# Window columns ahead of gate columns, SSD heads in a row, and banks of row blocks taken one by one, in a two-block kernel on one core

## What is computed

```python
h = modulate_2(rmsnorm(x, norm_mix), shift_m, scale_m)
proj = h @ w_in                                   # 512 pool | 1024 z | 1536 xbc | 16 dt
y_pool = pool_mixer(proj[pool], pool_w, pool_b, pool_scale)   # trailing means over 2, 4, 8, 16 tokens
y_ssd = ssd_mixer(proj[z], proj[xbc], proj[dt], ...)          # short convolution, 16 heads of 64
x = x + gate_m * (concatenate([y_pool, y_ssd]) @ w_out)
h = modulate_2(rmsnorm(x, norm_ffn), shift_f, scale_f)
x = x + gate_f * peer(h, w_query, sub_keys1, sub_keys2, expert_down, expert_up)
...
def pool_mixer(u, pool_w, pool_b, pool_scale):
    mixed = window_sum(u) / count - u
    return (einsum("bsgc,gcd->bsgd", mixed, pool_w) + pool_b) * pool_scale
def ssd_mixer(z, xbc, dt_raw, ...):
    y = ssd_chunked(xs * dt, dt * A, bs, cs) + xs * d_skip    # weights exp(decay) * (c . b) per head
    return rmsnorm(y * silu(z), ssd_norm)
```

## Time and profile before

| | before |
|---|---|
| median of 3 runs | 1455.42 us |
| profiled execution | 1453.92 us |
| its span, first to last instruction | 1452.1 us |
| mean granted TensorE clock | 0.986 |
| share of the span busy: PE, DVE, ACT, POOL | 96%, 71%, 57%, 45% |
| moved by DMA | 284 MB, 196 GB/s |

### The profile page before, as it was taken

The page is one execution under the profiler, slowest core; times in us unless marked ns, Lnnn a source line. Parts: engine busy times, 40 slices in busy tenths (PEclk is TensorE's granted clock), DMA queues, the critical chain, the costliest instruction groups (busy, mean ns, idle before and its releaser), DMA issues.

```text
span 1452.1 us, 31591 instructions
## 1 busy us (share of the span) xinstructions
PE 1400.9 (96%) x9822; PEld 1303.6 (90%) x9822; DVE 1032.7 (71%) x2231; ACT 823.5 (57%) x1602; POOL 649.0 (45%) x499
## 2 busy tenths in 40 slices
PE   5999999999999998999999999999999999999997
PEld 4799999999999968999999999999988888888886
DVE  6777768888867457429999468778775666666665
ACT  6668765555445554547887644334435555555554
POOL 4886791000016737688889866676640000000000
PEclk9999999999999989999999999999999999999999
DMA  8866575888963532564555544344435665655652
GB/s 311 302 230 220 199 264 198 321 318 308 343 238 129 177 106 94 186 224 166 186 183 180 176 141 143 133 144 137 137 126 177 193 196 189 194 195 189 194 194 87
DMA packets 79424, 284.31 MB, mean 196 GB/s; under 512 B 8836, under 2 KB 8964, under 8 KB 79240
## 3 DMA queue, kind: packets, MB, share of 16 engines
q1 hardware_dynamic: 79368, 283.59, 56.8%
HBM read 282.51 MB, written 1.05 MB: 195 GB/s over the span
## 4 chain that ended last, share of the span: by engine, by line
PE 39%; PEld 23%; issue 16%; POOL 16%; DVE 4%; ACT 2%; PEldq 1%; POOLq 0%; DMA 0%; SPq 0%; DVEq 0%; ACTq 0%
POOL w_lo L536 16%; PE psA L1689 9%; PE psA L1693 9%; PE psA L1692 9%; PEld psA L1693 6%; PEld psA L1689 5%; PEld psA L1692 5%; PEld psD L2139 3%; PE psD L1689 3%; PE psD L1692 3%; PE psD L1693 3%; PEld psD L1693 1%; PEld psD L1689 1%; PEld psD L1692 1%; DVE arena L1051 0%
## 5 line engine op out<-in xcount | busy, mean ns | idle before, releaser
L588 ACT CAST w_hi<-raw 128x512 fp32r<-128x512 f32 x872 | 535.3, 621 | 537.2 <-PE psA L1689 406.4
L536 POOL TENSOR_TENSOR w_lo<-raw,w_hi 128x512 fp32r<-128x512 f32 x484 | 642.2, 1345 | 413.9 <-ACT w_hi L588 401.0
L1689 PE MATMUL psA<-h_hi,w_hi 128*128 128x256 f32 x1568 | 453.4, 289 | 0.9 <-POOL w_lo L536 0.9
L1693 PE MATMUL psA<-h_hi,w_lo 128*128 128x256 f32 x1568 | 444.0, 283 | 0.0
L1692 PE MATMUL psA<-h_lo,w_hi 128*128 128x256 f32 x1568 | 444.0, 283 | 0.0
L1008 DVE TENSOR_TENSOR w_lo<-raw,w_hi 128x512 fp32r<-128x512 f32 x388 | 266.9, 691 | 159.5 <-ACT w_hi L588 158.6
L1689 PEld LDWEIGHTS psA<-h_hi,w_hi 128*128 128x128 f32 x1568 | 300.9, 192 | 4.6 <-issue 1.8
L1692 PEld LDWEIGHTS psA<-h_lo,w_hi 128*128 128x128 f32 x1568 | 301.3, 192 | 0.0
L1693 PEld LDWEIGHTS psA<-h_hi,w_lo 128*128 128x128 f32 x1568 | 300.9, 192 | 0.0
L1689 PE MATMUL psA<-w_hi,u_hi 128*128 128x512 f32 x512 | 200.5, 392 | 3.2 <-DVE u_lo L1065 3.2
L1693 PE MATMUL psA<-w_hi,u_lo 128*128 128x512 f32 x512 | 200.1, 391 | 0.0
(11 more groups left out here) (363 smaller groups left out, 2062.6 us busy)
## 6 DMA issues: line engine op xcount, KB each, us to landing
raw<-expert_down SPq DMA_DIRECT2D x128, 512.0 KB, 3.2
raw<-expert_up SPq DMA_DIRECT2D x128, 512.0 KB, 3.5
arena<-ada SPq DMA_DIRECT2D x96, 512.0 KB, 5.1
raw<-gateup SPq DMA_DIRECT2D x44, 512.0 KB, 5.1
raw<-feat SPq DMA_DIRECT2D x28, 512.0 KB, 3.8
raw<-win SPq DMA_DIRECT2D x24, 512.0 KB, 3.2
raw<-down SPq DMA_DIRECT2D x22, 512.0 KB, 6.1
raw<-wout SPq DMA_DIRECT2D x20, 512.0 KB, 4.2
```

The lines of the kernel that those rows point to most:

```text
L536: nc.gpsimd.tensor_tensor(w_lo[:, s * HALF:(s + 1) * HALF], raw[:, n % 8 * HALF:(n % 8 + 1) * HALF], w_hi[:, s * HALF:(s + 1) * HALF].bitc ...
L588: nc.scalar.copy(w_hi[:, n % SLOTS * HALF:(n % SLOTS + 1) * HALF], raw[:, n % 8 * HALF:(n % 8 + 1) * HALF]).then_inc(hi_ready, 1)
L1689: first = mm(o, w[0], m[0], start=start, stop=False, skip_group_check=True)
L1693: return mm(o, w[1], m[0], start=False, stop=stop, skip_group_check=True)
```

## The change

It has four parts. (1) In the first block the convolution of the second pair stands ahead of the reciprocal of the row chain, log1p_exp has one operation fewer, the last rows come behind the third pair, the exp of the row maxima moves on ACT to the head of softmax_exp, and gate_cols moves on PE from behind unit 8 to behind unit 15, with its copy on DVE behind m_decay. (2) row_blocks takes its banks one by one inside the first row block, and ssq_heads comes in the middle of the second row block. (3) ACT splits one half between the normalized blocks of the second block's first norm. (4) The pool columns come ahead of the gate columns. PE runs twelve units with dt_cols and turn_xs behind the first five and the four pooled products behind the last four; then all heads in a row, with two decays ahead of cb and two ahead of each pair. DVE computes sums and means beside the gate columns, and ssd_out writes its sum back to the PSUM bank. The inverse root of the heads goes to PSUM.

```diff
...
-Z2_Z, Z2_POOL = XBC, XBC + KC
+Z2_POOL, Z2_Z = XBC, XBC + NPOOL
...
-            stream(lambda u: win2[u], 24)
+            stream(lambda u: win2[u], XBC)
+            for j in range(NPOOL):
+                load(win2[XBC + KC + j])
 
             sp.wait_ge(d_drained, D_AT["down"] + 4)
             sp.dma_start(pool_wt, pool_w[:, :, :]).then_inc(sem("pool_w_in"), 16)
             sp.dma_start(keysT, keys[:, :, :]).then_inc(sem("keys_in"), 16)
+            stream(lambda u: win2[u + XBC], KC)
...
-            for j in range(2, 7):
+            for j in range(2, 8):
                 qk_bias(j)
-            act.wait_ge(sem("m_rows"), 1)
-            nc.scalar.activation(r_e[0:MH, :], r_t[0:MH, :], ACT.Exp, scale=-1.0).then_inc(sem("exp_m"), 1)
-            qk_bias(7)
...
+                if first == 0:
+                    act.wait_ge(sem("m_rows"), 1)
+                    nc.scalar.activation(r_e[0:MH, :], r_t[0:MH, :], ACT.Exp, scale=-1.0).then_inc(sem("exp_m"), 1)
...
+                act.wait_ge(sem("m_cols"), 1)
...
-            norm_modulated("ssq_both", xn2, mods[:, 1, 0:KC])
-
             next_stage()
-            split(1)
+            norm_modulated("ssq_both", xn2, mods[:, 1, 0:KC], split_behind=6)
+
+            split_half()
...
-            for j in range(KC):
-                if j < KC - 1:
-                    split(1)
-                A.free(nc.scalar.activation(z2T[:, Z2_Z + j, :], A.bank()[:, 0:T], ACT.Silu))
+            def upper_mix(j):
+                nc.scalar.copy(mix_hi[:, j, :], mixT[:, j, :]).then_inc(sem("mix_hi"), 1)
+
+            for j in range(NPOOL):
+                split(1)
+                A.free(nc.scalar.copy(z2T[:, Z2_POOL + j, :], A.bank()[:, 0:T]))
                 if j in (2, 3):
                     xbc_silu(XBC - 4 + j)
-
-            split(1)
+            for j in range(KC):
+                split(1)
+                A.free(nc.scalar.activation(z2T[:, Z2_Z + j, :], A.bank()[:, 0:T], ACT.Silu))
+                if j >= KC - NPOOL + 1:
+                    act.wait_ge(d_drained, D_AT["pool"] + j - (KC - NPOOL))
+                    upper_mix(j - (KC - NPOOL + 1))
...
-                if h % 2 == 0 and h // 2 < NPOOL:
-                    A.free(nc.scalar.copy(z2T[:, Z2_POOL + h // 2, :], A.bank()[:, 0:T]))
...
-                if h % 2 == 1 and h // 2 < NPOOL:
-                    split(1)
-
-            def upper_mix(j):
-                nc.scalar.copy(mix_hi[:, j, :], mixT[:, j, :]).then_inc(sem("mix_hi"), 1)
-
-            def upper_pool():
-                for j in range(NPOOL):
-                    act.wait_ge(d_drained, D_AT["pool"] + j + 1)
-                    upper_mix(j)
+                if h == 3:
+                    act.wait_ge(d_drained, D_AT["pool"] + NPOOL)
+                    upper_mix(NPOOL - 1)
+            next_stage()
+
             table_of_roots()
-            squares(mixT[:, NPOOL:MIXC, :], xn2, lambda k: (sem("ssd_y"), 2 * k + 2), "y_squares")
-            upper_pool()
+            squares(mixT[:, NPOOL:MIXC, :], xn2, lambda k: (d_drained, D_AT["ssd"] + 2 * k + 2), "y_squares")
+            split(1)
...
+                    inverse = rinv[:, :] if name != "ssq_ssd" else psA[:, A_AT[name] % BANKS, T:2 * T]
...
-            def log1p_exp(k, n, beside=None):
+            def log1p_exp(k, n, behind_sum, behind_error, behind_inverse=None):
+
 
                 V.scalar_tensor_tensor(out=r_abs[0:n, :], in0=r_f[0:n, :], scalar=-1.0, in1=r_f[0:n, :],
                                        op0=ALU.mult, op1=ALU.max).then_inc(sem("row_abs"), 1)
                 dve.wait_ge(sem("row_exp"), k + 1)
                 V.tensor_scalar(r_u[0:n, :], r_e[0:n, :], 1.0, None, ALU.add).then_inc(sem("row_u"), 1)
-                if beside:
-                    beside()
+                behind_sum()
                 dve.wait_ge(sem("row_u"), k + 1)
-                own(V.tensor_scalar(r_t[0:n, :], r_u[0:n, :], -1.0, None, ALU.add))
-                own(V.tensor_tensor(r_t[0:n, :], r_e[0:n, :], r_t[0:n, :], ALU.subtract))
+                own(V.scalar_tensor_tensor(out=r_t[0:n, :], in0=r_u[0:n, :], scalar=-1.0, in1=r_e[0:n, :],
+                                           op0=ALU.add, op1=ALU.subtract))
+                behind_error()
                 own(V.reciprocal(r_abs[0:n, :], r_u[0:n, :]))
+                if behind_inverse:
+                    behind_inverse()
                 own(V.tensor_tensor(r_t[0:n, :], r_t[0:n, :], r_abs[0:n, :], ALU.mult))
                 dve.wait_ge(sem("row_ln"), k + 1)
-                own(V.tensor_tensor(r_l[0:n, :], r_l[0:n, :], r_t[0:n, :], ALU.add))
+                own(V.tensor_tensor(r_l[0:n, :], r_l[0:n, :], r_t[0:n, :], ALU.subtract))
...
-            log1p_exp(0, MH, lambda: conv_qk(0))
-            conv_qk(2)
+            log1p_exp(0, MH, lambda: conv_qk(0), lambda: conv_qk(2))
...
+            conv_qk(4)
             V.tensor_tensor(r_t[R, :], r_abs[R, :], r_u[R, :], ALU.add).then_inc(sem("m_rows"), 1)
             V.tensor_scalar(r_f[R, :], r_u[R, :], -1.0, None, ALU.mult).then_inc(sem("neg_m"), 1)
-            conv_qk(4)
...
-            log1p_exp(1, SH, lambda: conv_pair(0, xbcT, "conv_w2", 0))
+            log1p_exp(1, SH, lambda: conv_pair(0, xbcT, "conv_w2", 0), lambda: None,
+                      lambda: conv_pair(2, xbcT, "conv_w2", 0))
             own(V.scalar_tensor_tensor(out=r_i[S, :], in0=r_f[S, :], scalar=0.0, in1=r_l[S, :],
                                        op0=ALU.max, op1=ALU.add))
-            conv_pair(2, xbcT, "conv_w2", 0)
...
             conv_pair(4, xbcT, "conv_w2", 0)
+            own(V.memset(inv_t[:, 0, :], 1.0))
+            own(V.tensor_tensor_scan(inv_t[:, 1, :], inv_t[:, 0, :], inv_t[:, 0, :], 0.0, ALU.add, ALU.max))
+            own(V.memset(pool_a[:, :, 0:16], 0.0))
+            own(V.memset(pool_b[:, :, 0:16], 0.0))
+            own(V.reciprocal(inv_t[:, 0, :], inv_t[:, 1, :]))
+            conv_pair(6, xbcT, "conv_w2", 0)
...
+            for g in range(NPOOL):
+                pool_sums(g)
+            pool_means()
+            for g in range(NPOOL):
+                Dr.free(V.tensor_scalar(mixT[:, g, :], Dr.bank()[:, 0:T], col("pool_b", g), col("pool_scale", g),
+                                        ALU.add, ALU.mult))
+                if g >= 1:
+                    lower_mix(g - 1)
...
+            def ssd_out(j):
+                b = Dr.bank()[:, 0:T]
+                own(V.scalar_tensor_tensor(out=b, in0=xbcT[:, j, :], scalar=col("d_skip", j), in1=b,
+                                           op0=ALU.mult, op1=ALU.add))
+                Dr.free(V.tensor_tensor(mixT[:, NPOOL + j, :], b, z2T[:, Z2_Z + j, :], ALU.mult))
...
+                if j == 2:
+                    lower_mix(NPOOL - 1)
...
-            def row_unit(banks, rhs, first, last, R):
+            def row_unit(banks, rhs, first, last, R, between=None):
 
                 for h in range(2):
                     w = half()
                     for k in range(4):
                         n = 4 * h + k
+                        if first and n % 2 == 0:
+                            banks.append(R.bank())
                         done = product(banks[n // 2][:, (n % 2) * T:(n % 2 + 1) * T],
                                        [part_[:, k * P:(k + 1) * P] for part_ in w], rhs,
                                        start=first and n % 2 == 0, stop=last, opens=k == 0)
                         if last and n % 2 == 1:
                             R.full(done)
-
-            def row_blocks(n, rhs, ready, behind_first=None):
-                banks = [Dr.bank() for _ in range(BANKS)]
-
-                def one(k, first=False, last=False):
+                    if between and h == 0:
+                        between()
+
+            def row_blocks(n, rhs, ready, in_second=None):
+                banks = []
+
+                def one(k, first=False, last=False, between=None):
                     pe.wait_ge(*ready(k))
-                    row_unit(banks, [part_[:, k, :] for part_ in rhs], first, last, Dr)
+                    row_unit(banks, [part_[:, k, :] for part_ in rhs], first, last, Dr, between)
                 one(0, first=True)
-                if behind_first:
-                    behind_first()
-                turns, rest = divmod(n - 2, 4)
+                one(1, between=in_second)
+                turns, rest = divmod(n - 3, 4)
                 with repeat(pe, turns, {halves: 8}) as i:
                     for j in range(4):
-                        one(i * 4 + (j + 1))
+                        one(i * 4 + (j + 2))
                 for j in range(rest):
-                    one(turns * 4 + 1 + j)
+                    one(turns * 4 + 2 + j)
...
-                if u == 8:
-                    gate_cols()
...
+                if u == 15:
+                    gate_cols()
...
+            def pooled(g):
+                pe.wait_ge(sem("pool_w_in"), 16)
+                pe.wait_ge(sem("pooled"), g + 1)
```

(40 more changed lines are left out.)

78 lines of the change are left out of this document (26 added, 52 removed).

## The result

The changed kernel takes **1440.26 us** (median of four runs, 1438.14 to 1442.91), against 1455.46 us (four runs, 1455.23 to 1457.16) for the kernel before on the same chip: a ratio of 0.9903 with a 95% interval of 0.9881 to 0.9924, 1.0% faster. The profiled execution took 1441.06 us around a span of 1439.3, at a mean granted clock of 0.991 (before 1452.1 and 0.986). That is inside the range by 0.3 us, 10.3 us under the forecast, and 0.4 from the 1440.7 of rival 1.

The account below looks back on a forecast made before the run. TensorE (PE), busy 96% of the span, was taken as the bound, so its waits and half clock count. -3.5 - 3.8 - 0.9 + 3.7 - 0.3 = -4.8 gave 1450.6 us; range 1440 to 1457.

Parts of the forecast that it names:

- rival 1: Heads: first pair waits under 1.5 us or the clock recovers, wout2 starts at full speed; 1440.7 us, chance 0.20.
- the prediction's own signs: It called itself wrong if the first pair waits under 1.5 us, or the clock is 1.00 in the heads.
- First block, -3.5: Row chain: earlier conv_qk(2) removes PE's 2.12 us bank wait and the half clock behind it; -3.5 us (0 to -3.8).
- Down projection, -3.8: Banks taken one by one remove PE's wait until 365.00 and half clock; -3.8 us (-1.5 to -3.8).
- Rival 3: Early waits replaced by waits for weights, clock falls anyway; about 5 of 7.3 us stay, 1455.6 us, chance 0.10.
- Convolutions, -0.9: Second block: conv_pair(6) ahead of DVE's idle time, conv_pair(2) into the row chain, shorten PE's wait; -0.9 us (0 to -1.4).
- Heads, +3.7: First unit behind the convolutions to wout2: late first pair, then heads at half clock; +3.7 us (+1.5 to +7).
- PE has by then ... waited 2.5: Step in the heads: PE idles 2.5 us ahead of the first pair, expected at about 528.0.
- w_out, -0.3: Stage wout2: fewer waits with the inverse in PSUM, against 2.1 us of half clock; -0.3 us (-2.5 to +1.5).
- Rival 2: POOL is shut out for each whole DVE operation, so PE waits for weights; 1455.8 us, chance 0.10.
- Rival 4: Heads in lockstep, each pair's exps awaiting the previous pair's read, 6.7 us instead of 3.95; 1470 us, chance 0.04.

Follow-up runs that it names:

- e_first: Changed kernel with conv_qk(2) behind all of log1p_exp and conv_qk(4) behind the last row operations again, in the first block; 1437.32 us.
- e_banks: Changed kernel with all four psD banks taken ahead of the first row block again, in both row_blocks; 1442.72 us.
- e_nosplit: Changed kernel without the half split inside the first norm of the second block (both halves behind it); 1434.33 us in one run.
- v2: Changed kernel with conv_pair(4) behind log1p_exp, memsets and reciprocal behind the last convolution, ssq_heads ending the second row block, earlier ACT half splits; 1430.34 us.
- e_two: Changed kernel with four extra DVE additions of two SBUF inputs ahead of the window sums, result not read; 1439.60 us in one run.
- e_late2: Changed kernel with four extra copies of 512 columns on ACT ahead of the first head's exps; 1450.72 us in one run.
- e_late1: Changed kernel with two extra copies of 512 columns on ACT ahead of the first head's exps; 1445.31 us in one run.
- e_sbuf: Changed kernel with ssd_out's sum and the heads' inverse root in SBUF, as before the change; 1447.79 us in one run.
- e_heads: Changed kernel without part (4): second block's units, heads, window sums and outputs as in the kernel before; 1449.05 us, ratio 0.9966 to the kernel before.

## Why the prediction was right and wrong

The measured time is in the range, yet by the prediction's own signs it was wrong: the first pair waited under 1.5 us, and the clock was 1.00 in the heads.

**First block, -3.5: right.** -4.3 at the place, the second convolution ahead of the reciprocal as said (89.8; forecast 88.7, or 89.7 with the 1.0 us by which this execution was late), no wait, full clock. By e_first, 1.0 of it is the order's own; the rest stands on the shorter chain (1.3) and on a fall of the clock that need not happen. In the 76 units that follow, all executions of the changed code are 0.8 to 1.1 us longer than before, with no new wait of PE: untraced.

**Down projection, -3.8: right at the place, not in the sum.** -3.2, by e_banks 1.9 for the order when the clock holds. What the forecast had wrong is "0" for the stages around: +1.3 for another pace and +1.9 in the norm, where the clock fell for 6.8 us and not 3.4. In the second profile of the changed kernel these are 0.0 and +0.5. So the 1.3 and 1.4 of the norm's 1.9 are the execution's, not the change's. The +0.5 goes with the changed code: all four of its profiles with 3.4 us at half clock in the norm and 3.4 in the xbc units have 16.7 to 16.8 there, and without the early half (e_nosplit) it is 16.33, against 16.21 before. Rival 3 gave such losses 0.10; it had new waits for weights as the cause, and there are none.

**Convolutions, -0.9: wrong by 1.1.** The bound 0 was nearer: PE still waits 1.22 us. The forecast took the idle time of DVE as what delays conv_pair(6); v2 shows that what stands ahead of the convolutions does: with conv_pair(4) right behind log1p_exp and the 2.9 us of memsets and reciprocal behind the last convolution both waits are gone. The changed kernel's trace tells the two edits apart: its wait of 1.22 us ends at 467.55, ahead of the first memset (467.81), and DVE had started conv_pair(4) only at 464.63, behind five row operations; the memsets can only have made the one of 0.34 at 473.89. The forecast had charged their 2.9 us to the idle time.

**Heads, +3.7: wrong, -9.7.** The step that failed is "PE has by then ... waited 2.5". In the frame of the changed execution (2.0 us earlier), forecast and measured are:
- copy and window sums 9.3 us, measured 8.1 (497.2 to 505.3): the copy took its own 0.68, and each of the four sums 0.97 to 0.99 us more than alone (2.20, 1.94, 1.67 and 1.41 instead of 1.23, 0.96, 0.68 and 0.42), not a whole POOL operation of 1.3;
- last mean done at 518.1, measured 515.7: seven at 1.43 us, forecast 1.44, but the eighth took 0.42 and the evictions behind it were quick. ACT had stood waiting for 2.97 us for the evicted pool product, so POOL had nothing to lower. The forecast had that wait of ACT, and did not draw from it that POOL falls idle and frees DVE. e_two shows the same on a larger scale;
- from there to the first pair 7.9, measured 8.2;
- the pooled product 0 was to be 1.5 us late; it came without a wait. Yet PE was ready at 523.4, forecast 523.5, since its own work was 1.3 us more than summed.

So the pair came 2.1 us earlier than forecast, PE on time, and 2.5 became 0.5. The next step, the clock behind a wait of 2.5, held in the one run that made such a wait, in size too: e_late2 measured 27.3 us at 0.50 and 3.95 us per pair. Of the 13.4 us between +3.7 and -9.7, the earlier pair is 2.2 and the run of heads 11.2 (27.7 us forecast, 16.5 measured from 523.89 to 540.35). That a wait of under 1.5 us keeps the clock, which rival 1 took from the earlier trace rows, holds as a tendency only: 1.55 lost it in e_late1, and 0.51 to 0.53 kept it in eight profiles and lost it in e_sbuf.

**w_out, -0.3: -1.3.** The forecast held 2.1 us against the stage for half clock at its start, which fell away with the clock kept; against that stands a wait of 1.19 of ssq_heads for POOL that it did not have. The gain from PSUM is there, as e_sbuf shows.

**The rivals.** Rival 1 (0.20) is nearest to what happened: a wait under 1.5 us, clock 1.00, 2.3 us between pairs, 18.4 us for the run of heads forecast and 16.5 measured. Its reason was not the one: ACT's chain was no quicker (8.2 us for 7.9), the last mean was 2.4 us earlier. That its time of 1440.7 is met within 0.4 us is luck. Its own terms give more than the 10 us it has (9.3 for the heads and 2.1 for half clock in w_out); the named stages brought 18.3 us instead of its 14.8, and 5.2 went elsewhere (+1.0, +1.0, +1.3, +1.9). Rival 2 did not come: at 485 to 520 PE has no wait for lowered weights. POOL did lose more than the forecast's 0.2 per operation: eleven of them took 17.57 us from 497.4 on, 1.60 each, where one alone takes 1.30:

```profile
497.42 17.57 POOL L530 TENSOR_TENSOR w_lo<-raw,w_hi 128x512 fp32r<-128x512 f32 x11 [0.59 <-ACT w_hi L582]
517.23 3.93 POOL L530 TENSOR_TENSOR w_lo<-raw,w_hi 128x512 fp32r<-128x512 f32 x3 [2.23 <-ACT w_hi L582]
```

That is 3.3 us lost, against 6.2 that sums (3.3) and seven means (2.9) take by themselves: about half, hidden by POOL's lead. The loss is not a share of each, though. Beside the sums, which alone take 1.23, 0.96, 0.68 and 0.42 us, POOL's operations took 2.28, 2.02, 1.75 and 1.48 instead of 1.29: 0.99, 0.73, 0.46 and 0.19 more, in each case DVE's own time less about 0.23. So long operations of DVE cost POOL nearly all that they take, and short ones half. The forecast had 0.15 from the short ones alone. The Trainium skill ("SBUF — State Buffer", section "Who interferes with whom") lets one of the two hold the shared port for its whole instruction. For DVE the trace agrees but for 0.3 us: 1.40 us for an operation of 0.42 beside one of 1.29. For POOL it agrees but for 0.23 us of each operation. The same section of the Trainium skill says that a VectorE instruction with at most one SBUF input does not contend with GpSimd; for the changed place of the inverse the runs agree, with 0.47 against 1.52 us. Rival 4 had no sign in the profile. Nor had the cause of rival 3, though more was given back in this execution (4.2 us) than the 2.3 of 7.3 that it said.

The chances were the right way round (faster 0.64). The range held the time by 0.3 us, and with luck: the six later runs of the changed kernel have a median of 1439.85 us, just outside. It came that near because the forecast named the one question that carried 10 us and gave the other answer a case of its own; the weight on the wrong answer (0.56) rested on a difference of two sums of 45 us, each good to about 1.5.

## What to carry to other kernels

Where a stretch of short, sparse matmuls follows a wait, price the clock with the wait: here 2 us of lateness cost 12.6, of which 10.5 is half clock that lasted through the heads. When two chains race over 45 us and a wait of 1 or 2 us decides, give both outcomes, and measure with an edit that moves the loser on purpose (four copies here). Contention between engines that feed each other stopped by itself here when one of them waited (e_two), so the price of one operation must not be multiplied by their number. And a difference of single profiles is to be taken by stage, against executions that were at half clock for as long in that stage.

## What the runs showed of the hardware that was not expected

- The same code with the same wait may or may not lose the clock: at 0.51 to 0.53 us ahead of the heads eight profiled executions kept it and e_sbuf lost it; behind the wait of 2.21 to 2.23 us for weights in the xbc units it fell in seven of ten; at 2.36 us ahead of the down projection it lost nothing in e_banks, at 2.12 it did in the kernel before. In e_heads it fell behind a wait of 0.67 us.
- Once lost ahead of the heads, the clock stayed at 0.50 for 23.9 to 27.3 us although PE's records show no idle time, with PEld busy for about 2 of 4 us; among units, with PEld busy throughout, falls lasted 3.4 or 6.8 us. It came back between 0.2 us ahead of the first unit of w_out (e_sbuf) and 1.4 us behind it (e_late2). What brings it back was not tried.
- Units of one code ran at 302 or 310 matmuls per 36 us at a granted clock of 1.00 throughout (2.88 or 2.81 us a unit), the slower in five of the thirteen profiled executions with the changed loop. What sets this pace stays open, and so does why v2 did not lose the clock in five runs.
